# Three modulation units of a two-block network are summed by VectorE in place, and TensorE multiplies the sums by ones

## The chip, the cores and the metric

The kernel runs on one core of one Trainium2 chip. The time is the device time of one execution in microseconds (us). A core has five engines that run side by side and wait for each other by counting semaphores: TensorE (matrix products, results in the PSUM memory), VectorE and ScalarE (element-wise work), GpSimd (little to do here) and SyncE, which issues most of the transfers from the chip's main memory, in a fixed order. 16 transfer engines carry them out.

## The reference, cut to what matters

Two transformer blocks run one after the other over 256 tokens of width 1024, all in float32. Each block has a recurrent or convolution branch, an attention branch and an expert layer with 32 experts, whose weights are most of the bytes. The change touches one small part of the first block, its modulation:

```python
def first_block(x, c, ...):
    cond = jax.nn.silu(c)                       # 1 x 1024
    mod = cond @ w_ada[l] + b_ada[l]            # w_ada: 1024 x 6144
    sh1, sc1, g1, sh2, sc2, g2 = jnp.split(mod[:, None, :], 6, axis=-1)
    h = rms_norm(x, norm1_gain[l]) * (1.0 + sc1) + sh1
    proj = h @ w_in[l]
    ...                                         # two branches on proj, merged
    x = x + g1 * (merged @ w_out[l])
    h2 = rms_norm(x, norm2_gain[l]) * (1.0 + sc2) + sh2
    x = x + g2 * moe_ffn(h2, ...)
```

`mod` is one row times a 24 MB matrix. Its last third (`sc2`, `g2`) is what the three units of this change work on. It isn't needed before the second half of the block.

## The kernel before, in words

All weights go through a ring of slots in SBUF, each 128 partitions x 4096 floats (2 MB). Ahead of the first expert layer the list `PRE_UNITS` (line 95) gives the order of the transfers and the slot of each: twelve modulation units ("ada", b, kp), ten units of the input projection ("in"), the two branches' output projections ("at", "hg") and two units of `w_out`. SyncE takes the list in this order and waits before each until the slot's last user is done (`unit_free`, line 246; for a modulation unit that is the semaphore `ada_done`, which TensorE counts up). So a unit that is late holds up all behind it.

Modulation unit ("ada", b, kp) holds 256 of the 1024 input rows (two blocks of 128, one per half of the slot) and 2048 output columns. Each of these input rows has to be weighted with its entry of `cond` and summed over the partitions. TensorE does this in `ada(n)` (line 1519): for each of the two blocks four products, each on 32 columns of its array, with `cond32` (the entry of `cond` copied 32 times) as weights and 512 columns of the slot as the moving operand. The eight products go to bank 7 of PSUM, and the four units of one b add up there. Units 8 to 11 make up b = 2, and after the last of them VectorE adds the bank to `modrow` (line 2188).

The work between is written out by hand, engine by engine. The input projection is done in "rounds", one for each unit: a float32 weight is split into an upper part (ScalarE, `split_upper`, line 356) and the rest (VectorE, `split_lower`, line 361), in halves of a unit called pieces, and TensorE does three products for each (`split_tokens`, `split_cols`). Rounds 5, 6, 7, 8 are pieces 9 to 16; TensorE waits for the semaphore `w_lower` before each piece. Between the rounds TensorE does attention and the chunk-wise recurrence: transposes of the attention weights `s` (line 1605, six groups of four, each into one of three PSUM banks that VectorE and ScalarE empty in turn, lines 2138 and 1295), the attention output, the scores of the chunks, and transposes for the states (line 1643).

VectorE's program has the same work in its own order. Each of its instructions whose result a later one of its own needs is followed by a wait for its own completion (`sig` and `L`).

Of the kernel before, what the change touches and what calls it, by code (L numbers as in the profile page):

```python
# [22 lines left out]
ALU = mybir.AluOpType  # L23
# [5 lines left out]
TT, KD = SEQ // P, D // P  # L29
# [70 lines left out]
PRE = [d for d, _ in PRE_UNITS]  # L100
# [11 lines left out]
def program(nc, t, out):  # L112
    ctx = ExitStack()
    with ctx:
# [5 lines left out]
        def S(name):  # L120
            if name not in sems:
                sems[name] = ctx.enter_context(nc.semaphore(name))
            return sems[name]
# [23 lines left out]
        def C(name):  # L147
            a, n = CONST[name]
            return consts[:, a:a + n]

        def sm(name, n=None):
            a, w = SMALL[name]
            return small[:, a:a + (n or w)]
# [7 lines left out]
        slots = [ring4[:, i, :] for i in range(4)] + [ring2[:, i, :] for i in range(2)] \  # L161
# [19 lines left out]
        def slot_of(u):  # L181
            if u < MOE1:
                return PRE_UNITS[u][1]
            if u < MID0:
                if u in EARLY_UNITS:
                    return None
                return (0, 1, 3, 2, 4, 5)[(u - MOE1) % NSLOT]
            if u < MOE2:
                return (0, 1, 3, 2)[(u - MID0) % 4]
            return (3, 2, 0, 1, 4, 5)[(u - MOE2) % NSLOT]  # L190

        SLOT_OF = [slot_of(u) for u in range(MOE2 + NSLOT)]
# [5 lines left out]
        def before_in_slot(u):  # L198

            return max(v for v in range(u) if SLOT_OF[v] == SLOT_OF[u])  # L200
# [25 lines left out]
        def loaded(u):  # L226

            return S(f"loaded{SLOT_OF[u]}"), 16 * SLOT_OF[:u + 1].count(SLOT_OF[u])
# [12 lines left out]
        ROUNDS = big_rounds()  # L241
        R2 = sum(1 for r in ROUNDS if r[0] < MID0)
        ADA = [n for n, d in enumerate(PRE) if d[0] == "ada"]
        IN0 = PRE.index(("in", 0))

        def unit_free(u):

            if u < MOE1 and PRE[u][0] == "ada":
                return S("ada_done"), ADA.index(u) + 1
            if MOE1 <= u < MID0:  # L250
# [20 lines left out]
        def wait(eng, sv):  # L271
            eng.wait_ge(sv[0], sv[1])
# [57 lines left out]
        def upper(n):  # L330

            m = n % 3
            return ring2_r[:, m // 2, 2048 * (m % 2):2048 * (m % 2) + 2048]\
                .rearrange("p (k n) -> p k n", k=PIECES[n][2].shape[1])
# [23 lines left out]
        def split_lower(v, n):  # L358
            v.wait_ge(S("w_upper"), n + 1)
            _, _, w, w_r = PIECES[n]  # L360
            nc.vector.tensor_tensor(w_r, w, upper(n), ALU.subtract).then_inc(S("w_lower"), 1)  # L361
# [561 lines left out]
        def _(sp):  # L923
# [7 lines left out]
            for u, d in enumerate(PRE):  # L931
                if slot_used(u):
                    wait(sp, unit_free(before_in_slot(u)))
                if u == IN0:
                    w = t["w_in"][0, :, IN_COLS[0][0]:IN_COLS[0][0] + 512].rearrange("(k p) n -> p k n", p=P)
# [175 lines left out]
        def _(pool):  # L1111
# [10 lines left out]
            nc.gpsimd.memset(at(A1MAP, "reset").rearrange("p (g j) -> p g j", g=16)[:, :, 0:1], 0.0).then_inc(S("reset"), 1)  # L1122
            wait(pool, loaded(IN0))
            small_load(sm("hg_gain"), bc(t["hg_norm_gain"][0]), "smalls")
# [317 lines left out]
        def _(pe):  # L1442
# [25 lines left out]
            def split_tokens(r, lo=(hT_low[:, 0:4, :], hT_low[:, 4:8, :]), ready=None, after_first=None):  # L1468

                o = PS[:, banks(r), :]  # L1470

                def product(j, parts, first, last):
                    nk, n = parts[0][1].shape[1:3]
                    for i in range(TT):
                        for k in range(nk):
                            for m, (a, w) in enumerate(parts):
                                ins = mm(o[:, i, 0:n], a[:, k, i * P:(i + 1) * P], w[:, k, :],
                                         first and k == 0 and m == 0, last and k == nk - 1 and m == 2)
                        if r in OUT_ENDS and last and i == 0:
                            ins.then_inc(S("half_done"), 1)  # L1480
                            after_first()
                    return ins
                if kind_of(r) == WHOLE:
                    split_products(r, product, (hT_up,), (hT_low,), ready)
                else:
                    split_products(r, product, (hT_up[:, 0:4, :], hT_up[:, 4:8, :]), lo, ready)
# [18 lines left out]
            def split_cols(r, up=hT_up, lo=hT_low, between=None):  # L1505

                o = PS[:, banks(r), :].rearrange("p b (c t) -> p (b c) t", c=2)

                def product(j, parts, first, last):
                    nk, nc_ = parts[0][1].shape[1], parts[0][1].shape[2] // P  # L1510
                    for c in range(nc_):
                        for k in range(nk):
                            for m, (a, w) in enumerate(parts):
                                ins = mm(o[:, nc_ * j + c, :], w[:, k, c * P:(c + 1) * P], a[:, k, :],
                                         k == 0 and m == 0, k == nk - 1 and m == 2)
                    return ins
                split_products(r, product, (up, up), (lo, lo), None, between)

            def ada(n):

                u = ADA[n]
                b, kp = PRE[u][1:]
                wait(pe, loaded(u))
                w = slots[SLOT_OF[u]].rearrange("p (k n) -> p k n", k=2)
                for kk in range(2):
                    k = 2 * kp + kk
                    for j in range(4):
                        last = nc.tensor.matmul(PS[32 * j:32 * j + 32, 7, :],  # L1528
                                                sm("cond32")[:, 32 * k:32 * k + 32], w[:, kk, 512 * j:512 * (j + 1)],
                                                start=k == 0, stop=k == KD - 1, tile_position=(0, 32 * j))  # L1530
                last.then_inc(S("ada_done"), 1)

            pe.wait_ge(S("first_consts"), 16)
# [53 lines left out]
            for g in range(2):  # L1587
                o = [aux_bank() for _ in range(2)]
                for j in range(2):
                    for r in range(2):  # L1590
                        last = att_score(o[r][:, j * 256:(j + 1) * 256], 4 * g + r + 2 * j, 1, 256)
                        if j == 1:
                            last.then_inc(S("aux_done"), 1)
            split_tokens(5)
            ada(9)
            split_cols(6)
            ada(10)

            s = at(A1MAP, "s").rearrange("p (h n) -> p h n", h=AH)
            pe.wait_ge(S("att_p"), 1)  # L1600
            for b in range(3):
                for r in range(2):
# [1 line left out]
                    for j in range(4):  # L1604
                        last = nc.tensor.transpose(o[:, j * P:(j + 1) * P], s[:, 4 * r + j, b * P:(b + 1) * P], ident)  # L1605
                    last.then_inc(S("aux_done"), 1)
            ada(11)

            pT0 = at(A1MAP, "pT0").rearrange("p (h q) -> p h q", h=AH)
            pT1 = at(A1MAP, "pT1").rearrange("p (h q) -> p h q", h=AH)  # L1610
# [3 lines left out]
            for r in range(2):  # L1614
# [5 lines left out]
                    last = mm(o[q, j // 2, P:256], vv[:, 1, kv], pT1[:, hh, :], False, True)  # L1620
                last.then_inc(S("aux_done"), 1)

            pe.wait_ge(S("hg_scores_in"), 1)
            o = aux_bank().rearrange("p (g i) -> p g i", g=8)
            qt = at(A1MAP, "qt").rearrange("p (g i) -> p g i", g=16)
            for g in range(8):
                for i in range(4):
                    n = SUB * (i + 1)
# [3 lines left out]
                                  qt[:, hc, SUB * i:SUB * i + SUB], True, True)  # L1632
            last.then_inc(S("aux_done"), 1)
            split_cols(7)

            pe.wait_ge(S("hg_kd"), 1)
            kd = at(A1MAP, "b").rearrange("p (h t) -> p h t", h=HH)
# [279 lines left out]
        def _(v):  # L1917
            count, aux = {}, [0]

            def sig(ins, name):  # L1920

                count[name] = count.get(name, 0) + 1
                ins.then_inc(S(name), 1)
                v.wait_ge(S(name), count[name])

            def L(ins):

                sig(ins, "v_step")

            def aux_bank():  # L1930
# [5 lines left out]
                v.wait_ge(S("aux_done"), r + 1)  # L1936
                return PS[:, 4 + r % 3, :]

            def begin(r):
                v.wait_ge(S("big_done"), r + 1)  # L1940
                return PS[:, banks(r), :]

            TS, TV, STT, CP = V.tensor_scalar, V.tensor_tensor, V.scalar_tensor_tensor, V.tensor_copy
# [50 lines left out]
            for j in range(2):  # L1994
                CP(sm("shiftT")[:, 4 * j:4 * j + 4], mT[:, 32 * j, :])
                last = STT(out=sm("scaleT")[:, 4 * j:4 * j + 4], in0=mT[:, 64 + 32 * j, :], scalar=1.0,
                           in1=cols[:, 28 + 4 * j:32 + 4 * j], op0=ALU.add, op1=ALU.mult)
# [17 lines left out]
            q, k, b, tmp = (at(A1MAP, n) for n in ("q", "k", "b", "tmp"))  # L2015
# [66 lines left out]
            for i in range(4):  # L2082
                n = SUB * (i + 1)
# [18 lines left out]
            for r in range(2):  # L2102
                o = aux_bank().rearrange("p (h n) -> p h n", h=4)
                sig(STT(out=s[:, r:8:2, 0:P], in0=o, scalar=HD ** -0.5, in1=bc_mid(wb[:, P:256], 4),
                        op0=ALU.mult, op1=ALU.add), "aux_free_V")
            for r in range(4):
# [3 lines left out]
                        op0=ALU.mult, op1=ALU.add), "aux_free_V")  # L2110
# [16 lines left out]
            split_lower(v, 11)  # L2127
            v.wait_ge(S("hg_exp"), 6)
            sig(TV(b, b, k, ALU.mult), "hg_kd")
            split_lower(v, 12)  # L2130
            v.wait_ge(S("att_exp"), 17)
            L(TV(sm("den"), sm("den"), sm("es"), ALU.add))
# [1 line left out]
            TV(s[:, :, 0:P], s[:, :, 0:P], bc_last(sm("den")[:, 0:8], P), ALU.mult)  # L2134
            sig(TV(s[:, :, P:384], s[:, :, P:384], bc_last(sm("den")[:, 8:16], 256), ALU.mult), "att_p")
            split_lower(v, 13)
            for n in range(0, 6, 2):
                sig(CP(pT_part(n), aux_bank().rearrange("p (h n) -> p h n", h=4)), "aux_free_V")
            for r in range(2):
# [22 lines left out]
            last.then_inc(S("hg_st"), 1)  # L2162
            v.wait_ge(S("hg_st"), 1)
            sig(V.memset(sm("ang"), 0.0), "aux_free_V")
            split_lower(v, 15)
            split_lower(v, 16)
            kdT = at(A1MAP, "kdT")
# [7 lines left out]
            for c in range(3):  # L2175
# [3 lines left out]
                else:  # L2179
                    for hh in range(HH):  # L2180
                        last = STT(out=states[:, c, hh, :], in0=states[:, c - 1, hh, :], scalar=decay[:, 4 * hh + c:4 * hh + c + 1],
                                   in1=o[:, hh, :], op0=ALU.mult, op1=ALU.add)
# [272 lines left out]
            for m in range(4):  # L2455
# [3 lines left out]
                w = [cols[:, 16 + 4 * j + m:17 + 4 * j + m] for j in range(3)]  # L2459
# [98 lines left out]
            for i in range(TT):  # L2558
                last = STT(out=INSIDE[:, i, :].rearrange("p (g e) -> p g e", g=4), in0=bc_last(LOST[:, i, :], 8), scalar=NEG,
                           in1=LG[:, i, 4:36].rearrange("p (g e) -> p g e", g=4), op0=ALU.mult, op1=ALU.add)  # L2560
# [52 lines left out]
```

## Time and profile before

| | |
|---|---|
| median of 3 runs | 1558.39 us (1557.97 to 1558.5) |
| the profiled execution | 1558.42 us |
| its span (first to last instruction) | 1556.6 us |
| TensorE busy | 1447.0 us, 93% |
| VectorE busy | 602.6 us, 39% |
| ScalarE busy | 342.8 us, 22% |
| GpSimd busy | 22.7 us, 1% |
| mean transfer rate | 382 GB/s, 594.63 MB |

The busy shares are means over stages with different limits. The stage of this change lies between 100 and 160 us; the experts of the first block run from about 250 us to beyond 1100 us. In the rows further down PE is TensorE's products, PEld its loading of weights, DVE is VectorE, ACT ScalarE, POOL GpSimd and SPq the queue of SyncE's transfers. `ring` is any of the slots, `arena` the working memory, `PS` the PSUM memory. Two kinds of product take two records per instruction, so 16 records of line 1528 are the eight products of one unit.

### The profile page before, as it was taken

What the parts mean: (1) busy time and instruction counts of PE and PEld (TensorE: products, weight loads), DVE (VectorE), ACT (ScalarE), POOL (GpSimd) and SP (SyncE); (2) the same over time, 40 slices, a digit from 0 to 9 for tenths busy, and PEclk for the clock granted to TensorE, in tenths of its full rate; (3) what the DMA queues carried; (4) which work ended last, traced back from release to release, by engine and by line L of the source; (5) the groups of instructions that cost most, each with busy time, mean ns of one, the idle gap of its engine ahead of it and who ended that gap; (6) DMA issues with size and microseconds to landing.
All of it is one profiled execution on the core that took longest, in us unless ns stands there. A gap on an engine that the chain in (4) does not pass through costs nothing.

```text
span 1556.6 us, 20902 instructions
## 1 busy us (share of the span) xinstructions
PE 1447.0 (93%) x8692; PEld 754.9 (48%) x8692; DVE 602.6 (39%) x920; ACT 342.8 (22%) x395; POOL 22.7 (1%) x36
## 2 busy tenths in 40 slices
PE   5999999999999999999998989999989999998677
PEld 2878985333333333333332333333338999854343
DVE  4686683232223232231321321323247687522111
ACT  4564332010101010110100100101033384321110
POOL 1100100000000000000000000000000000000000
PEclk9999999999999999999999999999999999999889
DMA  9986589999999999999999999999996446999998
GB/s 383 372 324 264 197 351 395 430 428 428 429 427 427 428 429 427 429 427 429 428 428 429 426 427 429 429 427 428 429 403 229 163 163 261 362 386 423 422 422 343
DMA packets 76385, 594.63 MB, mean 382 GB/s; under 512 B 5499, under 2 KB 6753, under 8 KB 36901
## 3 DMA queue, kind: packets, MB, share of 16 engines
q1 hardware_dynamic: 74000, 588.25, 91.5%
q0 software_dynamic: 1792, 4.86, 0.9%
q8 instruction: 48, 0.79, 0.2%
q10 hardware_dynamic: 532, 0.64, 0.1%
q14 instruction: 13, 0.10, 0.0%
HBM read 592.66 MB, written 1.06 MB: 381 GB/s over the span
## 4 chain that ended last, share of the span: by engine, by line
PE 60%; DMA 34%; DVE 3%; issue 1%; SPq 1%; ACT 1%; POOL 0%; DVEq 0%; ACTq 0%
PE PS L563 54%; DMA ring<-in_w_up 26%; DMA ring<-in_w_up_e 6%; PE PS L743 3%; DMA arena<-in_w_in 2%; DMA ring<-in_w_down_e 1%; PE PS L763 1%; PE PS L1528 1%; DVE ring_r L361 1%; DVE arena L853 1%; PE PS L679 1%; SPq L1093 1%; ACT ring_r L356 0%; POOL arena_r L1119 0%; PE PS L1605 0%
## 5 line engine op out<-in xcount | busy, mean ns | idle before, releaser
L563 PE MATMUL PS<-ring,arena 128*64 128x512 f32 x3020 | 671.2, 597 | 41.0 <-DMA ring<-in_w_up 28.7
L563 PEld LDWEIGHTS PS<-ring,arena 128*64 128x64 f32 x3020 | 212.3, 137 | 462.1 <-issue 400.1
L563 PE MATMUL PS<-arena 128*128 128x128 f32 (+12 forms) x1240 | 228.7, 441 | 2.9 <-DVE arena L2109 0.9
L841 DVE TENSOR_SCALAR arena<-PS 128x512 f32<-128x512 f32 x32 | 22.1, 692 | 482.6 <-PE PS L563 482.6
L542 ACT ACTIVATE arena<-arena 128x512 f32<-128x512 f32 x32 | 20.2, 630 | 698.5 <-DVE arena L841 698.5
L563 PE MATMUL PS<-ring_r 128*128 128x256 f32 (+1 forms) x576 | 171.6, 305 | 0.1
L563 PEld LDWEIGHTS PS<-arena 64*128 64x128 f32 (+6 forms) x1240 | 108.6, 164 | 120.4 <-issue 114.9
L563 PE MATMUL PS<-hT_r,ring_r 128*128 128x256 f32 x800 | 151.7, 286 | 0.3 <-DVE ring_r L361 0.3
L361 DVE TENSOR_TENSOR ring_r<-ring,ring_r 128x2048 fp32r<-128x2048 f32 x51 | 116.4, 2291 | 37.2 <-ACT ring_r L356 36.1
L563 PEld LDWEIGHTS PS<-hT_r,ring_r 128*128 128x128 f32 x800 | 127.8, 193 | 2.3 <-issue 1.4
L356 ACT ACTIVATE ring_r<-ring 128x2048 fp32r<-128x2048 f32 x51 | 97.2, 1912 | 104.6 <-PE PS L563 99.2
L563 PEld LDWEIGHTS PS<-ring_r 128*128 128x128 f32 x576 | 110.3, 192 | 5.2 <-DVE ring_r L2399 0.5
L563 PE MATMUL PS<-ring_r,hT_r 128*128 128x512 f32 (+1 forms) x336 | 99.3, 383 | 3.1 <-ACT hT_r L1212 1.7
L743 PE MATMUL PS<-ring,arena 128*32 128x256 f32 x896 | 61.6, 438 | 31.1 <-DMA ring<-in_w_up_e 24.4
L563 PEld LDWEIGHTS PS<-ring_r,hT_r 128*128 128x128 f32 x336 | 61.9, 188 | 18.4 <-issue 3.8
L835 DVE TENSOR_TENSOR x<-x,PS 128x2048 f32<-128x2048 f32 x31 | 70.6, 2278 | 0.0
L863 DVE TENSOR_TENSOR arena<-PS,arena 128x512 f32<-128x512 f32 x32 | 22.1, 691 | 118.3 <-PE PS L563 118.3
L743 PEld LDWEIGHTS PS<-ring,arena 128*32 128x32 f32 x896 | 32.1, 125 | 59.1 <-DMA ring<-in_w_up_e 23.6
L563 PE MATMUL PS<-arena_r,ring_r 128*128 128x256 f32 x352 | 45.2, 278 | 0.0
L853 DVE COPY arena<-PS 128x512 f32<-128x512 f32 x32 | 22.1, 691 | 55.7 <-PE PS L679 55.7
L563 PEld LDWEIGHTS PS<-arena_r,ring_r 128*128 128x128 f32 x352 | 43.2, 188 | 0.2 <-issue 0.2
L542 ACT ACT_TABLE_LOAD x31 | 39.8, 1283 | 1.1 <-issue 0.5
(382 smaller groups left out, 965.2 us busy)
## 6 DMA issues: line engine op xcount, KB each, us to landing
ring<-in_w_up SPq DMA_DIRECT2D x128, 2048.0 KB, 20.7
ring<-in_w_down SPq DMA_DIRECT2D x59, 2048.0 KB, 18.6
ring<-in_w_in SPq DMA_DIRECT2D x17, 2048.0 KB, 11.2
ring<-in_w_gate_e SPq DMA_DIRECT2D x14, 2048.0 KB, 19.3
ring<-in_w_down_e SPq DMA_DIRECT2D x13, 2048.0 KB, 20.1
ring<-in_w_up_e SPq DMA_DIRECT2D x13, 2048.0 KB, 19.0
ring<-in_w_ada SPq DMA_DIRECT2D x12, 2048.0 KB, 16.1
ring<-in_w_out SPq DMA_DIRECT2D x4, 2048.0 KB, 7.7
```

The source lines that it names most:

```text
L356: nc.scalar.activation(upper(n), PIECES[n][2], ACT.Copy).then_inc(S("w_upper"), 1)
L361: nc.vector.tensor_tensor(w_r, w, upper(n), ALU.subtract).then_inc(S("w_lower"), 1)
L542: nc.scalar.activation(sg, glu, ACT.Sigmoid, scale=1.702).then_inc(S(f"{X}_sg"), 1)
L563: return nc.tensor.matmul(o, w, m, start=first, stop=last)
L679: mm_ = nc.tensor.transpose(PS[:, 1, i * P:(i + 1) * P], actb[:, i * P:(i + 1) * P], ident)
L743: mm_ = nc.tensor.matmul(PS[q, 2 + i, 0:256], xg2[:, k * P + CAP2 * j:k * P + CAP2 * (j + 1)], moe2_weights(where, 2 * i + j // 2, j % 2, ...
L763: mm_ = nc.tensor.matmul(PS[q, b, :], aT2[:, kk * P + CAP2 * j:kk * P + CAP2 * (j + 1)], moe2_dst(where, 4 + j // 2)[:, 2 * (j % 2) + kk, ...
L835: V.tensor_tensor(xflat, xflat, PS[:, 4:8, :].rearrange("p b n -> p (b n)"), ALU.add).then_inc(S(f"{X}_added"), 1)
L841: V.tensor_scalar(glu.rearrange("p (kk b q) -> p kk b q", kk=4, b=2), hu[:, :, :, :, 0], 7.0, None, ALU.min)\
L853: V.tensor_copy(aT, PS[:, 1, :]).then_inc(S(f"{X}_aT"), 1)
L863: V.tensor_tensor(ye[:, 0:512], PS[:, 1, :], g2h, ALU.mult).then_inc(S(f"{X}_ye"), 1)
L1093: sp.dma_start(moe2_pair(2, i)[:, o, :].rearrange("p (k n) -> p k n", k=2)[:, kk, c], w[:, kk, :])\
```

## The change

For units 9, 10 and 11 VectorE now makes the weighted sum of the two blocks in the slot itself: block 0 times its entries of `cond` (one scalar per partition), then block 1 times its entries plus that. TensorE then takes one block in place of two, with ones in place of `cond32` as weights, and waits for VectorE's sum (`ada_summed`) and no longer for the transfer, for which VectorE waits. The three calls on TensorE are also moved: unit 9 from ahead of round 6 to behind it, unit 10 from there to behind the attention output, unit 11 from ahead of the attention output to behind round 7. The sums stand in VectorE's order behind the product for `hg_kd`, behind piece 13's split, and behind the masks of the chunk scores.

```diff
--- before.py
+++ after.py
@@ -241,6 +241,7 @@
         ROUNDS = big_rounds()
         R2 = sum(1 for r in ROUNDS if r[0] < MID0)
         ADA = [n for n, d in enumerate(PRE) if d[0] == "ada"]
+        ADA_SUMMED = (9, 10, 11)
         IN0 = PRE.index(("in", 0))
 
         def unit_free(u):
@@ -1520,14 +1521,19 @@
 
                 u = ADA[n]
                 b, kp = PRE[u][1:]
-                wait(pe, loaded(u))
                 w = slots[SLOT_OF[u]].rearrange("p (k n) -> p k n", k=2)
-                for kk in range(2):
+                summed = n in ADA_SUMMED
+                if summed:
+                    pe.wait_ge(S("ada_summed"), ADA_SUMMED.index(n) + 1)
+                else:
+                    wait(pe, loaded(u))
+                for kk in range(1 if summed else 2):
                     k = 2 * kp + kk
                     for j in range(4):
                         last = nc.tensor.matmul(PS[32 * j:32 * j + 32, 7, :],
-                                                sm("cond32")[:, 32 * k:32 * k + 32], w[:, kk, 512 * j:512 * (j + 1)],
-                                                start=k == 0, stop=k == KD - 1, tile_position=(0, 32 * j))
+                                                C("ones")[:, 0:32] if summed else sm("cond32")[:, 32 * k:32 * k + 32],
+                                                w[:, kk, 512 * j:512 * (j + 1)],
+                                                start=k == 0, stop=kp == 3 and (summed or kk == 1), tile_position=(0, 32 * j))
                 last.then_inc(S("ada_done"), 1)
 
             pe.wait_ge(S("first_consts"), 16)
@@ -1592,9 +1598,8 @@
                         if j == 1:
                             last.then_inc(S("aux_done"), 1)
             split_tokens(5)
+            split_cols(6)
             ada(9)
-            split_cols(6)
-            ada(10)
 
             s = at(A1MAP, "s").rearrange("p (h n) -> p h n", h=AH)
             pe.wait_ge(S("att_p"), 1)
@@ -1604,7 +1609,6 @@
                     for j in range(4):
                         last = nc.tensor.transpose(o[:, j * P:(j + 1) * P], s[:, 4 * r + j, b * P:(b + 1) * P], ident)
                     last.then_inc(S("aux_done"), 1)
-            ada(11)
 
             pT0 = at(A1MAP, "pT0").rearrange("p (h q) -> p h q", h=AH)
             pT1 = at(A1MAP, "pT1").rearrange("p (h q) -> p h q", h=AH)
@@ -1620,6 +1624,7 @@
                     last = mm(o[q, j // 2, P:256], vv[:, 1, kv], pT1[:, hh, :], False, True)
                 last.then_inc(S("aux_done"), 1)
 
+            ada(10)
             pe.wait_ge(S("hg_scores_in"), 1)
             o = aux_bank().rearrange("p (g i) -> p g i", g=8)
             qt = at(A1MAP, "qt").rearrange("p (g i) -> p g i", g=16)
@@ -1632,6 +1637,7 @@
                                   qt[:, hc, SUB * i:SUB * i + SUB], True, True)
             last.then_inc(S("aux_done"), 1)
             split_cols(7)
+            ada(11)
 
             pe.wait_ge(S("hg_kd"), 1)
             kd = at(A1MAP, "b").rearrange("p (h t) -> p h t", h=HH)
@@ -1935,6 +1941,16 @@
                 aux[0] += 1
                 v.wait_ge(S("aux_done"), r + 1)
                 return PS[:, 4 + r % 3, :]
+
+            def ada_sum(n):
+
+                u = ADA[n]
+                kp = PRE[u][2]
+                w = slots[SLOT_OF[u]].rearrange("p (k n) -> p k n", k=2)
+                wait(v, loaded(u))
+                L(TS(w[:, 0, :], w[:, 0, :], sm("cond")[:, 2 * kp:2 * kp + 1], None, ALU.mult))
+                sig(STT(out=w[:, 0, :], in0=w[:, 1, :], scalar=sm("cond")[:, 2 * kp + 1:2 * kp + 2], in1=w[:, 0, :],
+                        op0=ALU.mult, op1=ALU.add), "ada_summed")
 
             def begin(r):
                 v.wait_ge(S("big_done"), r + 1)
@@ -2127,6 +2143,7 @@
             split_lower(v, 11)
             v.wait_ge(S("hg_exp"), 6)
             sig(TV(b, b, k, ALU.mult), "hg_kd")
+            ada_sum(9)
             split_lower(v, 12)
             v.wait_ge(S("att_exp"), 17)
             L(TV(sm("den"), sm("den"), sm("es"), ALU.add))
@@ -2134,6 +2151,7 @@
             TV(s[:, :, 0:P], s[:, :, 0:P], bc_last(sm("den")[:, 0:8], P), ALU.mult)
             sig(TV(s[:, :, P:384], s[:, :, P:384], bc_last(sm("den")[:, 8:16], 256), ALU.mult), "att_p")
             split_lower(v, 13)
+            ada_sum(10)
             for n in range(0, 6, 2):
                 sig(CP(pT_part(n), aux_bank().rearrange("p (h n) -> p h n", h=4)), "aux_free_V")
             for r in range(2):
@@ -2162,6 +2180,7 @@
             last.then_inc(S("hg_st"), 1)
             v.wait_ge(S("hg_st"), 1)
             sig(V.memset(sm("ang"), 0.0), "aux_free_V")
+            ada_sum(11)
             split_lower(v, 15)
             split_lower(v, 16)
             kdT = at(A1MAP, "kdT")
```

TensorE's order from the end of round 6 to the start of the attention output, before (line 1528 is a modulation unit, line 1605 the transposes, `arena 64x256` the attention output):

```order
L563 MATMUL PS<-ring_r 128x256
L563 MATMUL PS<-hT_r,ring_r 128x256
L1528 MATMUL PS<-ring,small 32x512 x8
L1605 MATMUL PS<-consts,arena 128x128 x24
L1528 MATMUL PS<-ring,small 32x512 x8
L563 MATMUL PS<-arena 64x256
L563 MATMUL PS<-arena 64x128
```

and now (line numbers are 5 higher, and 1 higher at line 563):

```order
L564 MATMUL PS<-ring_r 128x256
L564 MATMUL PS<-hT_r,ring_r 128x256
L1533 MATMUL PS<-ring,consts 32x512 x4
L1610 MATMUL PS<-consts,arena 128x128 x24
L564 MATMUL PS<-arena 64x256
L564 MATMUL PS<-arena 64x128
```

One unit of four products stands where one of eight stood (it is unit 9 now, and was unit 10), and nothing stands between the transposes and the attention output.

TensorE's order where the attention output ends and the chunk scores (16 columns) begin, before:

```order
L563 MATMUL PS<-arena 64x256
L563 MATMUL PS<-arena 64x128
L563 MATMUL PS<-arena 16x16 x2
L563 MATMUL PS<-arena 32x16 x2
L563 MATMUL PS<-arena 48x16 x2
L563 MATMUL PS<-arena 64x16 x2
```

and now:

```order
L564 MATMUL PS<-arena 64x256
L564 MATMUL PS<-arena 64x128
L1533 MATMUL PS<-ring,consts 32x512 x4
L564 MATMUL PS<-arena 16x16 x2
L564 MATMUL PS<-arena 32x16 x2
L564 MATMUL PS<-arena 48x16 x2
```

Unit 10 has come between the two.

VectorE's order from piece 11's split (line 361) to the first copies of transposed attention weights (line 2138), with what each waits for, before:

```order
L361 TENSOR_TENSOR ring_r<-ring,ring_r 128x8x256 [waits w_upper,hg_scores_in]
L2129 TENSOR_TENSOR arena<-arena 128x1024 [waits hg_exp]
L361 TENSOR_TENSOR ring_r<-ring,ring_r 128x8x256 [waits w_upper,hg_kd]
L2132 TENSOR_TENSOR small<-small 128x16 [waits att_exp]
L2133 RECIPROCAL small<-small 128x16 [waits v_step]
L2134 TENSOR_TENSOR arena<-arena,small 128x8x128 [waits v_step]
L2135 TENSOR_TENSOR arena<-arena,small 128x8x256
L361 TENSOR_TENSOR ring_r<-ring,ring_r 128x8x256 [waits w_upper,att_p]
L2138 COPY arena<-PS 128x4x128 [waits aux_done]
L2138 COPY arena<-PS 128x4x128 [waits aux_done,aux_free_V]
```

and now, from the product behind piece 11's split on (line 361 is 362, line 2138 is 2156):

```order
L2145 TENSOR_TENSOR arena<-arena 128x1024 [waits hg_exp]
L1951 TENSOR_SCALAR ring<-ring,small 128x2048 [waits loaded0,hg_kd]
L1952 SCALAR_TENSOR_TENSOR ring<-ring,small 128x2048 [waits v_step]
L362 TENSOR_TENSOR ring_r<-ring,ring_r 128x8x256 [waits w_upper,ada_summed]
L2149 TENSOR_TENSOR small<-small 128x16 [waits att_exp]
L2150 RECIPROCAL small<-small 128x16 [waits v_step]
L2151 TENSOR_TENSOR arena<-arena,small 128x8x128 [waits v_step]
L2152 TENSOR_TENSOR arena<-arena,small 128x8x256
L362 TENSOR_TENSOR ring_r<-ring,ring_r 128x8x256 [waits w_upper,att_p]
L1951 TENSOR_SCALAR ring<-ring,small 128x2048 [waits loaded2]
L1952 SCALAR_TENSOR_TENSOR ring<-ring,small 128x2048 [waits v_step]
L2156 COPY arena<-PS 128x4x128 [waits aux_done,ada_summed]
```

A sum of two instructions stands ahead of piece 12's split, and another between piece 13's split and the first copy.

## Rows read from the trace of the kernel before

**Rows 1.** One long stretch of the experts, busy time of each engine (x instructions), clock, transfers

```profile
600.00:1100.00 500.00, 474.80 (x2198) 167.19 (x2196) 139.29 (x234) 55.94 (x72) 0.00 (x0) 0.99 1.01 428
```

**Rows 2.** SyncE's queue in order of time (start, us), and landings of the ring

```profile
112.74 2.25 SPq L224 DMA_DIRECT2D ring<-in_w_ada  x2
126.93 2.25 SPq L224 DMA_DIRECT2D ring<-in_w_in  x2
133.63 0.37 SPq L224 DMA_DIRECT2D ring<-in_w_attn_branch  x1
198.83 0.34 SPq L951 DMA_DIRECT2D ring<-in_w_up  x1
DMA to landing us min/median/max: 7.6/9.9/12.8
```

**Rows 3.** The chain that ended last, 112 to 154 us: start, us, what

```profile
112.46 2.30 DVE ring_r L361
114.76 0.14 issue
114.89 5.99 PE PS L563 x48
...
120.89 6.01 PE PS L563 x48
126.89 1.85 PE PS L1528 x16
128.75 2.97 PE PS L1605 x24
131.72 1.85 PE PS L1528 x16
133.57 20.23 PE PS L563 x256
```

**Rows 4.** VectorE in order of time: start, us, operation, idle time before it

```profile
114.67 1.22 DVE L2129 TENSOR_TENSOR arena<-arena 128x1024 f32<-128x1024 f32 x1
118.54 2.29 DVE L361 TENSOR_TENSOR ring_r<-ring,ring_r 128x2048 fp32r<-128x2048 f32 x1 [2.65 <-ACT ring_r L356]
124.69 2.29 DVE L361 TENSOR_TENSOR ring_r<-ring,ring_r 128x2048 fp32r<-128x2048 f32 x1
129.37 0.69 DVE L2138 COPY arena<-PS 128x512 f32<-128x512 f32 x1 [2.38 <-PE PS L1605]
145.71 2.29 DVE L361 TENSOR_TENSOR ring_r<-ring,ring_r 128x2048 fp32r<-128x2048 f32 x1
150.09 2.29 DVE L361 TENSOR_TENSOR ring_r<-ring,ring_r 128x2048 fp32r<-128x2048 f32 x1 [2.09 <-ACT ring_r L356]
```

**Rows 5.** VectorE's operations by form: busy us, mean ns of one, idle before

```profile
L361 DVE TENSOR_TENSOR ring_r<-ring,ring_r 128x2048 fp32r<-128x2048 f32 x14 | 32.1, 2291 | 13.4 <-ACT ring_r L356 13.1
L2109 DVE SCALAR_TENSOR_TENSOR arena<-PS,consts 128x512 f32<-128x512 f32 x4 | 2.8, 692 | 1.4 <-PE PS L563 1.4
L1965 DVE TENSOR_SCALAR arena<-x,small 128x1024 f32<-128x1024 f32 x2 | 1.5, 754 | 0.1
L2086 DVE TENSOR_SCALAR arena<-arena 128x1024 f32<-128x1024 f32 x1 | 0.7, 694 | 0.0
L2086 DVE TENSOR_SCALAR arena<-arena 128x512 f32<-128x512 f32 x1 | 0.4, 426 | 0.0
```

**Rows 6.** ScalarE in order of time: its last copy of transposed weights

```profile
131.75 0.60 ACT L1295 ACTIVATE arena<-PS 128x512 f32<-128x512 f32 x1 [0.34 <-PE PS L1605]
```

**Rows 7.** Three equal stretches around the fall of TensorE's clock

```profile
137.68:141.09 3.41, 3.41 (x92) 3.11 (x93) 3.24 (x5) 0.00 (x0) 0.00 (x0) 1.00 1.05 398
141.09:144.50 3.41, 3.41 (x18) 3.41 (x17) 3.32 (x6) 0.00 (x0) 0.00 (x0) 0.50 1.00 398
144.50:147.92 3.42, 3.42 (x31) 3.42 (x30) 3.30 (x7) 0.00 (x0) 0.00 (x0) 1.00 0.03 13
```

**Rows 8.** TensorE at an early modulation unit, in order of time

```profile
26.46 1.92 PE L1528 MATMUL PS<-ring,small 128*32 128x512 f32 x16 [3.05 <-DMA ring<-in_w_ada]
```

## The prediction

> **What bounds the kernel now.** I read the views in this order: busy time by long stretches, the queue of transfers, the chain of work that ended last from 90 to 160 us, and then VectorE's and ScalarE's timelines in the same stretch. From 600 to 1100 us, the heart of the first expert stage, the transfer engines are busy all the time (share 1.01, 428 GB/s) and TensorE is not quite [rows 1]: the length of that stage is its bytes. But its transfers can't begin before the slots are free, and those are freed by TensorE: the first weights of the experts that go by a product of the last rounds are issued at 198.83 us [rows 2], and SyncE issues nothing ahead of its turn. So whatever TensorE gains or loses before 198 us moves the stream of the experts and with it the end, one for one. The change lies at 112 to 157 us, and there the chain is the thing to read. It comes from VectorE (the split at 112.46 us), and from 114.89 us on it is TensorE without a gap to 153.80 us: the two halves of round 6 (5.99 and 6.01 us), modulation unit 10 (1.85), the 24 transposes of the attention weights (2.97), unit 11 (1.85), and 20.23 us of attention output, chunk scores and round 7 [rows 3]. Two joints of it are closer than they look. Unit 9 ends before 114.89 and costs nothing: TensorE waits there for the split that ends at 114.76. And the second half of round 6 starts at 120.89, right behind VectorE's next split, which starts at 118.54 after 2.65 us of idle time and takes 2.29 [rows 3, 4]. VectorE is thus a bound twice within 6 us.
>
> **TensorE's side.** A unit is now 4 products in place of 8. The 8 take 1.85 us [rows 3], so 4 take 0.93 us, up to 1.0 if something of the unit is fixed. Unit 9 saved nothing where it stood, since the wait to 114.89 stands there anyway; moved behind round 6 it is 0.93 us of new work on the chain. Unit 10 leaves 1.85 and comes back as 0.93 behind the attention output, unit 11 leaves 1.85 and comes back as 0.93 behind round 7. Alone, that is 3 × 0.93 − 2 × 1.85 = −0.9 us, and not the 2.8 us that halving three units suggests.
>
> **VectorE's side.** Each sum is a multiply of 128x2048 by a scalar and a multiply-add of 128x2048, each with a wait for its own result. No row has either at this width. The multiply: 694 ns at 1024 columns and 426 at 512, 268 per 512, so 694 + 536 = 1.23 us, and the one that takes its scalar from memory as here is 0.06 longer at 1024 (754), so 1.29 [rows 5]. The multiply-add with two tensors takes 692 ns at 512, and two tensors at 2048 take 2.29 (line 361), so 2.29 [rows 5]. With some 0.03 us behind each, a sum is 3.6 us. From below, both could run like the multiply (2.6 us); from above, both like the two-tensor form (4.6). I take 3.6.
>
> **First joint, 114.76 to 127 us.** Sum 9 starts when the product of line 2129 ends (114.67 + 1.22 = 115.89) and ends at 119.5. The gap that should cover it ends at 118.54 [rows 4]. The split behind it starts 0.95 late, ends at 121.7, and the second half of round 6 starts at 121.84 instead of 120.89: +0.95. It ends at 127.85, and unit 9 (its sum is long there) at 128.78. The transposes begin as before (128.75).
>
> **Second joint, 128 to 134.5 us.** The six groups of transposes share three banks, so group 4 has to wait until VectorE has emptied group 1. VectorE did that at 129.37, after 2.38 us of idle time [rows 4]. Now its work is 0.95 late (the split of 124.69 starts at 125.64), and sum 10 stands between that split and the first copy. What stands behind a split starts 2.2 us after it (line 2129 at 114.67, behind the split of 112.46 [rows 3, 4]), so sum 10 runs from 127.84 to 131.44; the copy ends at 132.13; TensorE starts group 4 some 0.14 later (the same step as 114.76 to 114.89 [rows 3]) at 132.27. Three groups at 2.97 / 6 = 0.495 are done at 133.75. ScalarE empties the last, 0.60 us [rows 6], 134.38, and the attention output begins at 134.51. Before, it began at 133.57, behind unit 11, which hid this last copy (131.75 + 0.60). So here, with the 1.85 us of unit 11 gone from the path, TensorE is still 0.94 us late.
>
> **The rest.** Attention output, scores and round 7: 20.23 us, plus units 10 and 11, 1.86. The next piece of the chain starts at 134.51 + 20.23 + 1.86 = 156.60 in place of 153.80: **+2.8 us**. Sum 10 is ready (131.44) for unit 10. Sum 11 follows the masks of the scores (145.71 + 1.9 = 147.6) and ends at 151.2; the two splits behind it (rows at 145.71 and 150.09, the second after 2.09 of idle time [rows 4]) end at 155.8, and round 8 wants them only at 160. The copies of line 2170 wait for TensorE in any case. Transfers: the last modulation unit was issued at once behind its neighbour from 112.74 on; now its slot is free at 128.8, and SyncE holds the two projection units (126.93 [rows 2]) behind it. Landings took 7.6 to 12.8 us [rows 2], so unit 11 is there by 141.6, ahead of 147.6. The projection unit behind it is split by ScalarE at some 142 instead of 135, for round 8 at 160. The attention branch's unit (133.63) is issued at 157 and used from 173 on. All of this is hidden. No queue of GpSimd is passed.
>
> Behind 157 us all is the same and moves with TensorE. The profiled execution took 1558.42 us, 0.03 over the median of 1558.39. 1558.42 + 2.8 = **1561.2 us**. The bounds of a sum's price: with 2.6 us the first gap is just filled (+0), copy 1 starts at 129.5, the output at 132.55, the total is +0.9. With 4.6 us the first joint gives +2.0, copy 1 starts at 133.5, the output at 136.6, the total is +4.9.
>
> **Rival A: the clock falls once more (slower).** TensorE is granted 0.50 of its clock at 141.09 to 144.50, after a stretch of 92 short matmuls in 3.41 us; in that time it did 18 matmuls of round 7, and 31 in the next equal stretch [rows 7]: a loss of 3.41 × 13 / 31 = 1.4 us. After the change there is a second thin stretch: from 130.3 to 134.5 TensorE does 12 transposes (1.5 us) and waits for the rest. If the clock falls there, the attention output runs at 1.2 GHz and the loss is again 1.4: +4.2 us, 1562.6. For it: one thin stretch does pull it down. Against: the transposes split the wait in pieces of 2.0 and 0.8 us, and the 16 products at 26.46 us, behind a wait of 3.05 us, took the 1.92 us of full clock [rows 8]. It decides if the stretch counts as idle. The Trainium skill ("TensorE: Matmul & The Clock Gate", Part 1) makes half clock the default that activity lifts, and its Terms price it at the throttled time × (1 − K/N), 1.7 us for such a stretch. The rows say 1.4, and the sum by the page would be +4.5.
>
> **Rival B: the clock doesn't fall at all.** Unit 10 now stands between attention output and scores, and its products are as wide as those of the rounds at full clock. If that keeps the clock up at 141 us, 1.4 comes back: +1.4, 1559.8. Against: the scores themselves stay in one piece.
>
> **Rival C: VectorE's sums are hidden (faster).** If both sums fit (2.6 us or less and the copies in time), TensorE keeps its −0.9 and with B's 1.4 it is −2.3, 1556.1; to pass −3.1 something unseen must help. The gaps of 2.65 and 2.38 us stand against it.
>
> **Rival D: more is late.** Sums at the upper price: +4.9, 1563.3.
>
> **Chances.** My case (+2.8, itself 1.8 to 3.9) 47%, A 27%, B 12%, D 6%, C or any other way below no change 8%. 0.2% is 3.1 us, about what a measurement of this kernel can tell. My case lies just inside it: about two fifths of it fall outside. Slower by over 0.2%: 0.19 + 0.25 + 0.06 = 0.50 less a little for A below its size, 0.49. Faster by over 0.2%: 0.05, of C. Within: 0.46. For 8 in 10 the range is 1558.2 to 1563.6; the likeliest case's own is 1560.2 to 1562.3.
>
> **What would show it.** In the profile after: TensorE idle for some 2.2 us ahead of round 6 (112.7 to 114.9, waiting for the split); the second half of round 6 at 121.8; the multiply at 1.29 and the multiply-add at 2.29 us; the fourth group of transposes at 132.3, released by VectorE's copy; attention output at 134.5; the transposes of line 1643 (now 1649) at 156.6; the first expert weights at 201.6. I am wrong if the split at 118.54 isn't late, if the copy at 131.4 isn't what the transposes wait for, or if the shift at 157 us isn't found again at 201 and at the end.

## The result and the profile after

The changed kernel takes 1563.11 us (median of 20 runs, 1559.19 to 1565.87), against 1558.41 (20 runs, 1555.75 to 1561.78) for the one before beside it. The ratio is 1.0028, 95% interval 1.0022 to 1.0035: 4.4 us slower, between 3.4 and 5.5 (the two medians as they stand are 4.7 us apart). The forecast was 1561.2 with a range of 1558.2 to 1563.6. The result lies inside that range, and 0.8 us above the likeliest case's own, 1560.2 to 1562.3.

What answers to the two joints of [rows 3, 4] is first TensorE in order of time, only the pieces ahead of which it was idle (start, us, operation, idle time before and who ended it):

```profile
114.72 0.36 PE L564 MATMUL PS<-hT_r,ring_r 128*128 128x256 f32 x1 [2.20 <-DVE ring_r L362]
121.79 0.39 PE L564 MATMUL PS<-hT_r,ring_r 128*128 128x256 f32 x1 [1.10 <-DVE ring_r L362]
132.26 1.53 PE L1610 MATMUL PS<-consts,arena 128*128 128x128 f32 x12 [1.99 <-DVE arena L2156]
134.52 2.84 PE L564 MATMUL PS<-arena 128*64 128x256 f32 x32 [0.73 <-ACT arena L1296]
```

All four waits stand within 0.2 us of where the prediction put them (114.89, 121.84, 132.27, 134.51). The first was unit 9's free place. The second is sum 9's overhang, the third sum 10 ahead of VectorE's copy, the fourth ScalarE's last copy, which unit 11 used to hide.

Then the chain that ended last, of the same kernel (start, us, what; pieces called `issue`, all under 0.1 us here, are left out):

```profile
115.74 1.30 DVE ring L1951
117.06 2.36 DVE ring L1952
119.45 2.29 DVE ring_r L362
...
125.60 2.29 DVE ring_r L362
127.89 1.21 DVE ring L1951
129.13 2.36 DVE ring L1952
131.51 0.70 DVE arena L2156
132.26 1.54 PE PS L1610 x12
133.82 0.61 ACT arena L1296
134.52 2.84 PE PS L564 x32
137.37 0.99 PE PS L1533 x8
138.36 15.83 PE PS L564 x223
154.18 1.00 PE PS L1533 x8
155.18 0.60 PE PS L1649 x4
```

The chain of before was TensorE alone from 114.89 us on. This one runs through two of VectorE's sums, 9 (115.74 to 119.45) and 10. A halved unit costs 0.99 to 1.00 us here, against 1.85 for a whole one [rows 3]. And attention output, scores and round 7 take 2.84 + 15.83 = 18.67 us where they took 20.23: the clock did not fall in this execution. VectorE's operations by form (count, busy us, mean ns) and SyncE's first issue for the experts:

```profile
L1952 DVE SCALAR_TENSOR_TENSOR ring<-ring,small 128x2048 f32<-128x2048 f32 x3 | 7.1, 2351 | 0.1
L1951 DVE TENSOR_SCALAR ring<-ring,small 128x2048 f32<-128x2048 f32 x3 | 3.9, 1285 | 0.1
```

```profile
200.36 0.34 SPq L952 DMA_DIRECT2D ring<-in_w_up  x1
```

The issue at 200.36 answers to 198.83 [rows 2]: 1.5 us late, as are the state transposes (155.11 for 153.64). The prediction had 201.6 and 156.6 for the chain's 155.18: both came 1.2 to 1.4 us earlier, since it left the clock's fall in. This execution took 1559.19 us, the fastest of the 20, and only 0.8 us more than the profiled one of before. So a single profile of each kernel shows 1.5 us at the first issue where the medians differ by over 4, and the experiments had to say why. A single total says little, too: from that first issue to the end the fourteen profiled executions of this study took 1358.8 to 1362.6 us, with no order by kernel.

The yardstick below is **the stretch**: from the start of round 6's first product to the start of the first state transpose, both read from TensorE's timeline. Behind it almost nothing differs: from there to the issue that was at 198.83 the fourteen profiles show 45.19 to 45.26 us, but for one of 45.48, which is told below.

### The profile page after: what moved, and what is told of

The parts are those of the page before. It is cut to its first block, busy times and chain, and to the rows that moved or that the text cites. A ratio compares the mean times of both kernels' runs of the same rounds, so it can differ in the third digit from the quotient of the medians.

```text
span 1557.3 us, 20863 instructions
## 1 busy us (share of the span) xinstructions
PE 1442.2 (93%) x8668; PEld 752.2 (48%) x8668; DVE 613.3 (39%) x926; ACT 343.0 (22%) x395; POOL 22.7 (1%) x36
## 4 chain that ended last, share of the span: by engine, by line
PE 54%; DMA 39%; DVE 4%; SPq 1%; issue 1%; ACT 1%; POOL 0%; DVEq 0%; ACTq 0%
PE PS L564 48%; DMA ring<-in_w_up 31%; DMA ring<-in_w_down_e 4%; DMA ring<-in_w_up_e 3%; PE PS L744 2%; DMA arena<-in_w_in 2%; PE PS L764 1%; DVE ring_r L362 1%; PE PS L1533 1%; SPq L1094 1%; DVE arena L854 1%; PE PS L680 1%; ACT ring_r L357 0%; DVE ring L1952 0%; POOL arena_r L1120 0%
```

## Experiments

The first four ran on one chip, 12 runs each, beside 35 runs of the kernel before (median 1558.69). `...` in a diff marks lines left out.

**The moves alone.**

```diff
-        ADA_SUMMED = (9, 10, 11)
+        ADA_SUMMED = ()
...
-            ada_sum(9)
...
-            ada_sum(10)
...
-            ada_sum(11)
```

> The three units stand where the change puts them in TensorE's order, but each has its eight products, and VectorE makes no sums. My account: unit 9 behind round 6 is 1.85 us that was free in the wait for the split, and unit 10 has left that place, so the transposes begin as before; the attention output begins some 1.1 us earlier than behind unit 11 (132.5 for 133.57, since it now waits for ScalarE's last copy), and units 10 and 11 add 3.7. From the start of round 6 to the state transposes: 2.6 us more than before at equal clock, total about 1561.0. The rival that VectorE's sums are the whole cost and the moves free: 1558.4. The rival that clock falls are most of the measured +4.7: with the units dense between attention output and scores the clock falls less often, so under 1560.5 even with 2.6 us of added path.

Measured: 1562.25 us, ratio 1.0025 (1.0014 to 1.0036), and a stretch of 39.85 us at full clock. The chain (`issue` pieces left out again):

```profile
115.69 11.99 PE PS L564 x96
127.68 1.85 PE PS L1533 x16
129.53 2.98 PE PS L1610 x24
132.54 0.61 ACT arena L1296
133.24 2.84 PE PS L564 x32
136.08 1.85 PE PS L1533 x16
137.93 15.83 PE PS L564 x223
153.76 1.85 PE PS L1533 x16
```

Round 6 runs through without a gap, and three whole units stand on the chain where before there were two. Against 37.26 us for the kernel before at full clock (below) that is 2.6 us, the number expected. The median is 1.2 us above the 1561.0 expected, though; the section on the prediction comes back to that. So the moves cost nearly all of what the change costs, and halving the products, with the sums beside it, gives back nothing: 40.39 − 39.85 is 0.5 us worse. "VectorE's sums are the whole cost" (1558.4) falls, and so does the rival of the clock (under 1560.5).

**Sum 10 behind the copies.**

```diff
...
             split_lower(v, 13)
-            ada_sum(10)
             for n in range(0, 6, 2):
                 sig(CP(pT_part(n), ...), "aux_free_V")
+            ada_sum(10)
```

> The change, but sum 10 stands behind VectorE's three copies of transposed attention weights. My account: the fourth group of transposes no longer waits for VectorE (it waited 1.99 us), the attention output begins near 132.6, sum 10 ends at about 135.8 and unit 10 waits 0.3 us for it: 1.6 us off the change at equal clock, about 1561.5. If the thin stretch there also pulls the clock down in many runs (rival A), more comes off: 1560.3 or below. If the wait isn't on the path that sets the end: 1563.1.

Measured: 1562.40 us, ratio 1.0018 (1.0008 to 1.0029). Its stretch is 40.31 us with a fall of the clock at 140.8, which made 17.20 us of the 15.83 of scores and round 7. Less this 1.4 it is 38.9, 1.5 off the change, where I expected 1.6: the wait of 1.99 us was on the path. The ratios are 0.0010 apart, 1.6 us, but their intervals overlap. The median is 0.9 above the 1561.5 expected and 2.1 above rival A's 1560.3: that the thin stretch pulls the clock down in many runs is not borne out here.

**The waits filled.**

```diff
                     last.then_inc(S("aux_done"), 1)
+                    if (b, r) == (1, 0):
+                        wait(pe, round_free(6))
+                        keep_warm(2, 0)
+                    if (b, r) == (2, 1):
+                        keep_warm_short(2, 0)
```

> The change, with two wide products into an idle PSUM bank between the third and fourth group of transposes and two short ones behind the sixth (their results are not used), so that TensorE is busy in its two waits of 1.99 and 0.73 us. The waits themselves stay as long. My account with the waits as the main cost: the same time, 1563.1 within 0.5. Rival A, a fall of the clock in that thin stretch in most runs at 1.4 us each: 1561.9 or below, and a higher mean granted clock. If the added products delay the transposes: up to 0.3 us more.

Measured: 1563.05 us, ratio 1.0023 (1.0013 to 1.0032). TensorE (start, us, operation, idle before) between the third group of transposes and the attention output:

```profile
129.75 1.15 PE L1610 MATMUL PS<-consts,arena 128*128 128x128 f32 x9
130.73 1.88 PE L564 MATMUL PS<-consts 128*128 128x512 f32 x4
132.89 1.53 PE L1610 MATMUL PS<-consts,arena 128*128 128x128 f32 x12 [0.28 <-DVE arena L2161]
134.25 0.61 PE L564 MATMUL PS<-consts 128*128 128x128 f32 x4
```

The wait is busy now, and the median is the same. The clock still fell, at 142.0 near the end of the scores, for 6.8 us (stretch 43.20). Rival A's 1561.9 or below didn't come, and neither did its higher granted clock: 0.983 in the mean over these 12 runs and over the 20 of the change. One profile can't tell whether the filled waits spare a fall ahead of the attention output: it is weak evidence against rival A as a fall in most runs, and no remedy.

**Unit 9 back, sum 10 late.**

```diff
-        ADA_SUMMED = (9, 10, 11)
+        ADA_SUMMED = (10, 11)
...
             split_tokens(5)
+            ada(9)
             split_cols(6)
-            ada(9)
...
-            ada_sum(9)
             split_lower(v, 12)
...
-            ada_sum(10)
             for n in range(0, 6, 2):
                 sig(CP(pT_part(n), ...), "aux_free_V")
+            ada_sum(10)
```

> Unit 9 is back ahead of round 6 with eight products and without a sum, sum 10 stands behind VectorE's copies, units 10 and 11 as in the change. My account: nothing is late at the second half of round 6, the transposes begin at 126.9, the attention output at about 130.7 to 131, and units 10 and 11 cost 2.0 us behind it (in place of 3.7 ahead), with up to 0.4 of wait for sum 10: 0.5 to 0.9 us less path than before, about 1557.7. If the halved units cost as much as whole ones: 1559.5. If something behind 157 us is what made the change slow: above 1561.

Measured: 1559.54 us, ratio 1.0005 (0.9996 to 1.0013). The stretch is 36.70 us at full clock, 0.6 below the kernel before. TensorE's two waits in it after round 6:

```profile
130.68 2.84 PE L564 MATMUL PS<-arena 128*64 128x256 f32 x32 [0.73 <-ACT arena L1296]
134.00 1.07 PE L1533 MATMUL PS<-ring,consts 128*32 128x512 f32 x8 [0.48 <-DVE ring L1952]
```

This is the one profile with 45.48 us behind the stretch: VectorE is still busy with round 8's splits when the first state transposes are done, and the products behind them wait 0.67 us for it, 0.44 in the others. In the runs nothing of the 0.6 is left; it doesn't beat the kernel before, and its median is just the 1559.5 of the rival that a halved unit costs as much as a whole one. The chain speaks against that rival: the halved units take 0.99 us. It is 3.6 us faster than the change, and its stretch is 3.7 us shorter at full clock: unit 9's 1.0, the late split's 1.1 and the 1.6 of sum 10 ahead of the copies. So both joints and unit 9's place are what the change lost.

**The first joint alone undone.** One execution of this:

```diff
-        ADA_SUMMED = (9, 10, 11)
+        ADA_SUMMED = (10, 11)
...
             split_tokens(5)
+            ada(9)
             split_cols(6)
-            ada(9)
...
-            ada_sum(9)
             split_lower(v, 12)
```

> The change, but unit 9 is back ahead of round 6 with eight products and no sum; sum 10 stays ahead of VectorE's copies. This undoes the first joint alone. My account: the second half of round 6 isn't late and unit 9's 1.0 us is gone from behind it, 1.95 us together; but VectorE reaches the copies only 0.95 earlier than in the change, so the fourth group of transposes waits for it still, and the attention output begins only 0.9 earlier. From the start of round 6 to the state transposes: 39.5 to 39.6 us at full clock, for 40.4 in the change. The rival that the joints add up independently: 38.4.

Measured: 42.24 us, with the clock at half from 132.3 to 139.1. In the chain (`issue` pieces left out, of which one, ahead of 135.55, is 0.73 us):

```profile
131.39 0.70 DVE arena L2155
132.13 2.69 PE PS L1610 x12
135.55 4.61 PE PS L564 x32
140.16 0.99 PE PS L1533 x8
```

The three groups of transposes take 2.69 us for 1.54, the attention output 4.61 for 2.84. Less these 2.9 us it is 39.3, nearer to my 39.5 than to the rival's 38.4: the joints don't add up, since behind the first VectorE is the bound of the second. And this is a fall where rival A put it, though in a kernel whose wait is longer: TensorE had waited 3.13 us ahead of these transposes, for 1.99 in the change, and the clock fell.

**More profiles of both kernels.** One execution with profile each, three of before and four of the change, which the expectations call looks. With the first profile of each they are numbered B1 to B4 (before) and C1 to C5 (the change) behind the expectations.

> The kernel before, unchanged, for a second look at its clock. In its first profile the clock fell at 141 us and cost 1.4 us of round 7; from the start of round 6 to the state transposes it took 38.75. Two theories of the 1.0 to 1.6 us by which the change and the other variants are slower than their paths at equal clock: (F) that fall comes only in some executions of the kernel before, so that this profile was a slow draw: then this look shows 37.3 to 37.5 us. (G) it comes in nearly all of them and the excess lies elsewhere: 38.7 again.

> The kernel before again. F: 37.3 to 37.5 us from the start of round 6 to the state transposes in most of the looks. G: 38.7 in nearly all.

> The kernel before again. F: 37.3 to 37.5 us from the start of round 6 to the state transposes in most of the looks. G: 38.7 in nearly all.

> The change, unchanged, for a second look at its clock; from the start of round 6 to the state transposes its first profile took 40.4 us, without a fall of the clock. Four looks at the kernel before gave 38.75 three times (one fall at 141 us, 1.5 us) and 37.26 once. Theory A: in the change the thin stretch of 130 to 134 us pulls the clock down in many executions, ahead of or beside the fall after the chunk scores; then looks show 42 to 43.5 us where it does (attention output over 4 us for 2.84) and the mean over the looks is over 3.5 us above the mean of before (38.4). Rival: the falls are the same as before, 40.4 or 41.9, mean 3.0 above.

> The change again. Theory A: 42 us or more in about half of the looks. Rival: 40.4 or 41.9.

> The change again. Theory A: 42 us or more in about half of the looks. Rival: 40.4 or 41.9.

> The change again. Theory A: 42 us or more in about half of the looks. Rival: 40.4 or 41.9.

The stretch in each, read from TensorE's timeline, and the falls of the clock in it from the granted clock (a plain table):

```
B1 (rows above)   38.75   one fall, at 141.1, 3.4 us long
B2                38.75   at 140.3, 3.4 us long
B3                37.26   none
B4                38.75   at 140.8, 3.4 us long
C1 (shown above)  40.39   none
C2                43.24   at 142.0, 6.8 us long
C3                41.82   at 115.2 (start of round 6) and at 142.5, 3.4 us each
C4                41.91   at 116.1 (in round 6) and at 143.4, 3.4 us each
C5                43.26   at 135.2, 6.8 us long
```

The kernel before shows its fall in three of four: nearer to theory G (nearly all) than to F (few). The means are 38.4 and 42.1, a difference of 3.7 us; at full clock it is 40.39 − 37.26 = 3.1. Of C2 and C5 the granted clock (the second to last group of columns: clock, share of the transfer engines, GB/s), first of C2:

```profile
137.50:142.00 4.50, 4.50 (x112) 3.37 (x108) 4.19 (x8) 0.28 (x1) 0.00 (x0) 1.00 1.05 393
142.00:148.80 6.80, 6.80 (x60) 6.65 (x57) 6.52 (x14) 1.91 (x1) 0.00 (x0) 0.50 0.79 290
```

and of C5:

```profile
128.00:135.00 7.00, 5.00 (x43) 3.79 (x42) 6.40 (x5) 2.10 (x3) 0.00 (x0) 1.00 0.50 172
135.05:141.90 6.85, 6.12 (x39) 4.20 (x41) 2.36 (x5) 3.38 (x4) 0.00 (x0) 0.51 1.03 405
```

with its chain:

```profile
133.83 1.59 PE PS L1610 x12
...
136.15 5.41 PE PS L564 x32
141.56 1.22 PE PS L1533 x8
142.78 15.83 PE PS L564 x224
```

In C2 the fall begins near the end of the chunk scores, about where it does in [rows 7], but it is twice as long: it costs 2.8 us of scores and round 7. In C5 it comes after 7 us in which TensorE was busy for 5.00, and it takes the attention output from 2.84 to 5.41 us. The same stretch of C1, where the clock did not fall behind it, looks much alike (4.79 us busy of 7):

```profile
127.00:134.00 7.00, 4.79 (x39) 3.35 (x38) 6.37 (x6) 2.39 (x4) 0.00 (x0) 1.00 0.58 207
```

The kernel before showed no fall of 6.8 us here in four profiles. Theory A expected 42 us or more in about half of the change's further executions. Two of C2 to C5 are above 42, and the means are 3.7 apart where it said over 3.5. But only C5 has the fall that theory A is about, with the attention output over 4 us; in C2 that took 2.84. As an account of most executions, theory A is not shown.

## Why the prediction came out as it did

**Right: what bounds the kernel.** What is lost before the experts' first transfer arrives at the end. The part from the state transposes to the experts' first issue is unchanged, and the variants' ratios rise with their stretches: 0.6 us below before at full clock gave 1.0005, 1.7 above it 1.0018, 2.6 above it 1.0025, 3.1 above it 1.0028. Each is about 1.2 us more than its stretch says (see Open).

**Right: TensorE's side.** Unit 9 cost nothing where it stood. The moves alone give 2.6 us, and halving three units is worth no more than it takes away. The halved unit costs 0.99 us for my 0.93, so it has about 0.13 us that doesn't halve; two of them on the path make +0.1.

**Right: the two joints.** The late split (1.10 us of wait for my 0.95) and the copy behind sum 10 (1.99). The operations of a sum take 1.285 and 2.351 us for 1.29 and 2.29, and from its start to the next instruction's a sum takes 3.71 (115.74 to 119.45) for 3.6: +0.2 over two sums. With both corrections 2.8 becomes 3.1, and the stretch says 3.1 at full clock. Rival D's total, 1563.3, is the nearest to the measured one, but by its number only: it asked for sums of 4.6 us.

**Mis-sized: the clock.** I left its term at zero in the likeliest case and gave a further fall as rival A, at 27% and 1.4 us, and its absence as B, at 12%. Neither is a fixed state. The falls come and go from one execution to the next, in the kernel before too, and the median holds something like their mean: 1.1 us over the profiles of before (three of four, 1.49 each), 1.7 over those of the change (0, 2.85, 1.43, 1.52, 2.87). That is 0.6 us of the 1.6 that 2.8 falls short of 4.4, on nine profiles only, and with such a spread it may be chance. The granted clock of whole executions can't confirm it: it is 0.983 in the mean over the 20 runs of the change and 0.982 over the 35 of before, and most of the time at half clock lies behind this stage. I had taken the profile's fall at 141 us as part of the kernel.

The place of rival A was right in one of five profiles of the change (C5) and in the first-joint run. Its price was too low, since the time at half clock is twice as long there (2.9 us in both). My argument against it, the 16 products at 26.46 us that ran at full clock behind a wait of 3.05 us [rows 8], held for that one execution. The same products in C5:

```profile
26.76 3.64 PE L1533 MATMUL PS<-ring,small 128*32 128x512 f32 x16 [3.06 <-DMA ring<-in_w_ada]
```

B happened as well: C1 has no fall, but neither has B3, so unit 10 between output and scores isn't shown to be its cause.

**Open.** 3.7 of 4.4 us are accounted for, which is within the interval. But what is missing looks alike in kernels that differ: against before at full clock the ratios are 1.1 to 1.3 us more than the stretch for the moves alone, for sum 10 late, for unit 9 back and for the change (each interval is 1 to 1.7 us to either side). With the waits filled it is 0.5, if that profile's fall is priced as C2's. Falls of the clock in the change's thin stretch don't explain it in all four. One part can be seen ahead of round 6, where all these kernels are the same: it starts at 114.74 to 115.05 in the four profiles of before and at 115.12 to 116.28 in nine of the ten of the change and the variants (114.72 in C1). In the mean it is 0.5 us later in the change than before. A fall near 26 us, in one profile of before and in eight of the ten others, goes with most of the late starts, but sum 10 late starts at 115.21 without one. It was not tried whether that is more than chance or what would cause it.

The Trainium skill ("TensorE: Matmul & The Clock Gate", Terms) prices a fall at the throttled time × (1 − K/N), where K of N clock pulses pass. By that page the fall of C2 would cost an estimated 3.4 us, and the run shows 2.8; the 3.41 us of [rows 7] would cost an estimated 1.7, and the profiles of before show 1.49. The Trainium skill (the same page, Part 1) says that the same kernel meets a different number of slow products from run to run at its start. Here falls in the middle of a kernel differ too: before's stretch took 38.75 us three times and 37.26 once.

## What to carry to other kernels

Work that stands in a wait is free, and halving it gains nothing; moving it out of the wait costs all of it. Before giving an idle engine something in a gap, compare the gap with the work (2.65 us for 3.6 here), and look at what its next instruction releases: two gaps of one engine in a row are one budget, not two. And where a few us matter and TensorE's clock falls in the stretch, take the profiles of several executions of both kernels before a fall is booked on either side.

## What the runs showed of the hardware that I had not expected

The clock's falls move between executions of one program: the same round 7 ran at half clock for 3.4 us in three profiles of four (B1, B2, B4) and at full clock in the other (B3). A fall of 3.4 us there cost 1.5 us, one of 6.8 us cost 2.8 (C2). A fall can also be free: in C3 it began 0.1 us ahead of round 6's first product (115.34), and the slower first half filled the wait of 1.1 us for VectorE's split. There is no gap between the halves; unit 9 starts 13.15 us behind the start of round 6, for 13.02 in C1, and the fourth group of transposes 17.55 us behind it, for 17.54.
